# Half of the modulation's weight sums moved from TensorE to VectorE, the norms' squares added up before TensorE sees them, and GpSimd's subtraction cut in four

## The reference, cut to what matters

```python
c_act = silu(c)                                  # [1, 1024]
mod = c_act @ w_ada + b_ada                      # [1, 9216]
sh1, sc1, g1, sh2, sc2, g2, sh3, sc3, g3 = split(mod, 9)
u = rmsnorm(h, norm_ffn1) * (1 + sc1) + sh1
h = h + 0.5 * g1 * swiglu(u, w_ffn1_up, w_ffn1_down)     # f1, f1d
u = rmsnorm(h, norm_mix) * (1 + sc2) + sh2
h = h + g2 * hybrid_mixer(u, ...)                        # convolutions, gated delta rule
u = rmsnorm(h, norm_ffn2) * (1 + sc3) + sh3
h = h + 0.5 * g3 * swiglu(u, w_ffn2_up, w_ffn2_down)     # f2, f2d
h = rmsnorm(h, norm_final)
# second network: differential attention, squared-relu MLP m0, mLSTM, MLP m1, each behind an rmsnorm
# rmsnorm(x, w) = x / sqrt(mean(x * x) + 1e-6) * w
```

## Time and profile before

| | |
|---|---|
| median of 3 runs | 1561.55 us (1560.59 to 1565.43) |
| the profiled execution | 1560.52 us, its span 1558.4 us |
| TensorE busy | 1454.0 us, 93% of the span |
| VectorE busy | 977.7 us, 63% |
| ScalarE busy | 713.5 us, 46% |
| GpSimd busy | 536.7 us, 34% |
| DMA | 258 MB, 166 GB/s in the mean |

### The profile page before, as it was taken

One profiled execution on the slowest core, in us unless ns is written; L12 is line 12 of the kernel. 1 busy time (PEld: TensorE's weight loads), 2 busy tenths in 40 slices (PEclk: granted clock), 3 DMA queues, 4 the chain that ended last, 5 costly groups with the idle time before them and its releaser, 6 DMA issues.

```text
span 1558.4 us, 27943 instructions
## 1 busy us (share of the span) xinstructions
PE 1454.0 (93%) x12009; PEld 1299.8 (83%) x12009; DVE 977.7 (63%) x1301; ACT 713.5 (46%) x1122; POOL 536.7 (34%) x209
## 2 busy tenths in 40 slices
PE   6999999879888899899999989799999998899998
PEld 3888787868777888878888989688999996888998
DVE  4565545868865446575765477569944754789632
ACT  3544534533344334445555546445534455455432
POOL 0444432212121212334444333235543440345542
PEclk9999999979999999999999999899999997999999
DMA  9877676613233443357555544335565551355551
GB/s 360 270 236 254 232 268 198 154 55 116 78 109 137 137 136 109 135 170 238 189 186 191 189 136 150 108 104 186 177 210 168 158 164 53 106 161 185 197 169 49
DMA packets 234441, 258.16 MB, mean 166 GB/s; under 512 B 8457, under 2 KB 211663, under 8 KB 234319
## 3 DMA queue, kind: packets, MB, share of 16 engines
q1 hardware_dynamic: 230272, 252.35, 48.8%
q10 hardware_dynamic: 4047, 4.04, 1.4%
HBM read 253.75 MB, written 2.62 MB: 165 GB/s over the span
## 4 chain that ended last, share of the span: by engine, by line
PE 77%; DVE 15%; ACT 4%; issue 2%; DMA 1%; POOL 0%; DVEq 0%; SPq 0%; ACTq 0%
PE ps L665 30%; PE ps L659 23%; PE ps L661 11%; DVE w_lo L1707 2%; PE ps L632 2%; DVE mt L1907 2%; DVE sil L1907 2%; PE ps L917 2%; PE ps L695 1%; ACT w_hi L1177 1%; DVE cac L2376 1%; DMA raw<-in_w_ada 1%; PE ps L891 1%; PE ps L641 1%; PE ps L880 1%
## 5 line engine op out<-in xcount | busy, mean ns | idle before, releaser
L614 POOL TENSOR_TENSOR w_lo<-raw,w_hi 128x1024 fp32r<-128x1024 f32 (+1 forms) x204 | 536.2, 2630 | 1004.1 <-ACT w_hi L1177 1004.1
L1177 ACT CAST w_hi<-raw 128x1024 fp32r<-128x1024 f32 (+1 forms) x408 | 412.7, 1044 | 205.3 <-PE ps L665 138.5
L659 PE MATMUL ps<-u_hl,w_hi 128*128 128x512 f32 x1216 | 429.6, 398 | 3.9 <-DVE w_lo L1707 1.4
L665 PE MATMUL ps<-u_hl,w_hi 128*128 128x256 f32 x1856 | 364.0, 297 | 23.1 <-DVE w_lo L1707 4.5
L1707 DVE TENSOR_TENSOR w_lo<-raw,w_hi 128x1024 fp32r<-128x1024 f32 x204 | 280.7, 1378 | 134.3 <-ACT w_hi L1177 133.3
L661 PE MATMUL ps<-u_hl,w_lo 128*128 128x256 f32 x1216 | 340.3, 280 | 0.0
L665 PEld LDWEIGHTS ps<-u_hl,w_hi 128*128 128x128 f32 x1856 | 304.3, 201 | 36.7 <-issue 13.9
L659 PEld LDWEIGHTS ps<-u_hl,w_hi 128*128 128x128 f32 x1216 | 228.8, 188 | 66.1 <-issue 11.5
L665 PE MATMUL ps<-u_hl,w_lo 128*128 128x256 f32 x928 | 270.7, 292 | 0.0
L661 PEld LDWEIGHTS ps<-u_hl,w_lo 128*128 128x128 f32 x1216 | 230.0, 189 | 0.1
L665 PEld LDWEIGHTS ps<-u_hl,w_lo 128*128 128x128 f32 x928 | 186.6, 201 | 0.0
(11 more groups left out here) (365 smaller groups left out, 1687.1 us busy)
## 6 DMA issues: line engine op xcount, KB each, us to landing
raw<-in_mlp_w SPq DMA_DIRECT2D x64, 1024.0 KB, 5.2
raw<-in_w_ffn_up SPq DMA_DIRECT2D x44, 1024.0 KB, 5.1
raw<-in_w_ada SPq DMA_DIRECT2D x36, 1024.0 KB, 7.3
raw<-in_w_in SPq DMA_DIRECT2D x30, 1024.0 KB, 5.0
raw<-in_w_ffn_down SPq DMA_DIRECT2D x16, 1024.0 KB, 5.4
raw<-in_attn_w_in SPq DMA_DIRECT2D x12, 1024.0 KB, 4.9
raw<-in_mlstm_w_in SPq DMA_DIRECT2D x12, 1024.0 KB, 5.1
raw<-in_w_ffn_down SPq DMA_DIRECT2D x8, 768.0 KB, 4.2
```

The costliest lines, as they stand in the source:

```text
L614: pool.tensor_tensor(w_lo[half][:, 0:k, :], src, w_hi[half][:, 0:k, :].bitcast(F32), ALU.subtract).then_inc(low_ready(n, h)[0], 1)
L659: pe.matmul(two(b - 10 + m), x, z, start=(first and kt == ks.start), stop=False, skip_group_check=True)
L665: mm = pe.matmul(bank(b)[:, m * S:(m + 1) * S], a, z[c] if type(z) is tuple else z[:, c, :], start=(first and m == 0 and kt == ks.start an ...
L1177: act.copy(w_hi[t % HALVES][:, 0:k, :], src).then_inc(hi_ready, 1)
```

## The change

There are three parts.

**1. Nine pairs on VectorE.** For pairs 4 to 11 and 17 (`BY_VECTOR`) TensorE no longer makes `ada_sums`. VectorE forms the same sum in `rows(p, a)`: for each of the four blocks of a transfer it multiplies a 128 x 512 piece of `raw` by one column of `cpad` and adds it to `arow`, four dependent instructions per transfer. TensorE's `mod_sums` then waits for `row_sums` in place of ScalarE's copy, and SyncE waits for `row_sums` before it refills the buffer. In the up steps pair p is now due one step earlier (`ADA`: steps 0, 2, 4, 6, 8), its first half is added up in that step, the second in the next, and `mod_sums` follows in the one behind.

**2. Squares added by VectorE.** `summed(name, c)` adds the squares of blocks 2c, 2c + 1 into those of blocks 0, 1. TensorE then sums two blocks for `attn`, `mlp0`, `mlstm` and `mlp1`, and four (0, 1, 6, 7) for `ffn1`, `mix`, `ffn2` and `final2`, all in one place, behind the last group or behind the next stage's first slab.

**3. GpSimd in four pieces.** The subtraction of a half slab, one instruction of 128 x 1024, becomes four of 128 x 256.

```diff
@@ Plan.ada
-        self.group("ada", p)
+        if p not in BY_VECTOR:
+            self.group("ada", p)
@@ 
-ADA = {"f1": ({1: 4, 3: 5, 5: 6, 7: 7, 9: 8}, {0: 9, 1: 10, 2: 11, 3: 12}, {1: 9, 2: 10, 3: 11, 4: 12}),
+ADA = {"f1": ({0: 4, 2: 5, 4: 6, 6: 7, 8: 8}, {0: 9, 1: 10, 2: 11, 3: 12}, {1: 9, 2: 10, 3: 11, 4: 12}),
        "f2": ({1: 17}, {}, {})}
+BY_VECTOR = (4, 5, 6, 7, 8, 9, 10, 11, 17)
+BY_TENSOR = (2, 3, 0, 1, 12, 13, 14, 15, 16)
@@ SyncE, load
-                        sp.wait_ge(s("ada_sums"), 2 * turn(m // 2) + m % 2 + 1)
+                        p, a = divmod(m, 2)
+                        if p in BY_VECTOR:
+                            sp.wait_ge(s("row_sums"), 2 * BY_VECTOR.index(p) + a + 1)
+                        else:
+                            sp.wait_ge(s("ada_sums"), 2 * BY_TENSOR.index(p) + a + 1)
@@ GpSimd
-                    pool.tensor_tensor(w_lo[half][:, 0:k, :], src, w_hi[half][:, 0:k, :].bitcast(F32),
-                                       ALU.subtract).then_inc(low_ready(n, h)[0], 1)
+                    for kt in range(k):
+                        op = pool.tensor_tensor(w_lo[half][:, kt, :], src[:, kt, :], w_hi[half][:, kt, :].bitcast(F32),
+                                                ALU.subtract)
+                    op.then_inc(low_ready(n, h)[0], 1)
@@ TensorE, ffn
-                    if i in ups:
-                        ada_sums(ups[i])
-                    if i - 1 in ups:
-                        mod_sums(ups[i - 1])
+                    if i - 2 in ups:
+                        mod_sums(ups[i - 2])
...
-                    if g:
-                        squares(then, g - 1)
                     if g in mods:
                         mod_sums(mods[g])
-                    if g in downs:
+                    if g == 3 and g in downs:
                         ada_sums(downs[g])
                 if then not in LATE:
-                    squares(then, 3)
+                    squares(then)
@@ VectorE
+            def rows(p, a):
+                r = arrived(dve, ("ada", 2 * p + a))
+                if a == 0:
+                    dve.wait_ge(s("mod_sums"), turn(p) - 1)
+                row = row_at(p)
+                for k in range(4):
+                    x, c = raw4[r][:, k, :], cpad[:, 4 * a + k, 0:1]
+                    op = (dve.scalar_tensor_tensor(row, x, c, row, mul, add) if a or k else
+                          dve.tensor_scalar(row, x, c, None, mul))
+                    if k < 3:
+                        link(op)
+                op.then_inc(s("row_sums"), 1)
+                dve.wait_ge(s("row_sums"), 2 * BY_VECTOR.index(p) + a + 1)
...
+            def summed(name, c):
+                if c == 0 or c == 3 and name not in LATE[:-1]:
+                    return
+                dve.wait_ge(s("sq_ready"), 4 * NORMS.index(name) + c + 1)
+                op = dve.tensor_tensor(uf[:, 0:2, :], uf[:, 0:2, :], uf[:, 2 * c:2 * c + 2, :], add)
+                if name == "attn":
+                    op = dve.tensor_tensor(sq2[0], sq2[0], sq2[c], add)
...
@@ VectorE, ffn
                     dve.tensor_tensor(mt, sil, sil2, mul).then_inc(s("mid_f"), 1)
+                    if i in ups:
+                        rows(ups[i], 0)
                     if i - 1 in ups:
-                        mod_out(ups[i - 1])
+                        rows(ups[i - 1], 1)
+                    if i - 2 in ups:
+                        mod_out(ups[i - 2])
...
                         ahead(plan.slab[(name + "d", g, q)])
+                        if q < 2 and g and g - 1 in downs:
+                            rows(downs[g - 1], q)
...
+                        if q == 2 and g:
+                            summed(then, g - 1)
@@ VectorE, attention
                 ahead(plan.slab[("aqkv", 0)] + 1)
+                summed("attn", 3)
                 root("attn")
```

More of the change, by code:

```diff
@@ L684, in warm, with squares @@
                     pe.matmul(bank(7), cs("ident"), cst[:, 0:512], start=True, stop=True, skip_group_check=True)
-            def squares(norm, c):
+            def squares(norm):
                 v = NORMS.index(norm)
-                pe.wait_ge(s("sq_ready"), 4 * v + c + 1)
-                for k in (2 * c, 2 * c + 1):
+                pe.wait_ge(s("sum_ready"), v + 1)
+                for k in (0, 1) if norm in LATE[:-1] else (0, 1, 6, 7):
+                    if k == 6:
+                        pe.wait_ge(s("sq_ready"), 4 * v + 4)
+                    last = k == (1 if norm in LATE[:-1] else 7)
                     if norm == "final2":
@@ L730, in columns @@
                     if due and j == 0:
-                        squares(due, 3)
-                    if then and j:
-                        squares(then, j - 1)
+                        squares(due)
                 if pair:
@@ L771, in _ @@
             ada_sums(3)
-            for c in range(4):
-                squares("ffn1", c)
+            squares("ffn1")
             pe.wait_ge(s("params_in"), 16 * NPAR)
@@ L1071, in attention @@
                     if i == 0:
-                        squares("attn", 3)
+                        squares("attn")
                 for part in range(2):
@@ L1087, in attention @@
                             out_turned(1)
-                        elif c:
-                            squares("mlp0", c - 1)
             def mlstm():
@@ L1159, in _ @@
             mlp("m1", "mlp1", "final2")
-            squares("final2", 3)
+            squares("final2")
             turned_out(3)
@@ L1849, in _ @@
                 square(c)
+            for c in (1, 2):
+                summed("ffn1", c)
             dve.wait_ge(s("prm_T"), 1)
```

39 lines of the change are left out of this document (24 added, 15 removed).

## The result

| | median | runs | profiled span | TensorE clock |
|---|---|---|---|---|
| before, beside it | 1561.55 us | 3 | 1558.4 us | 0.963 |
| after | 1595.7 us | 4 | 1592.8 us | 0.957 |

The ratio is 1.0222, interval 1.0203 to 1.0241: 2.2% slower, against a forecast of 1557 us and a range up to 1583. A fourth run of before, at 3551.66 us, was disturbed and is left out.

What follows compares the result with a forecast made beforehand. TensorE, 93% busy, was taken to bound the kernel. Terms +11 (ups), +8 (downs), +2 (second network), -11.5 (squares), -14 (pieces) sum to -4.5 on 1560.52 us: 1556, stated as 1557 against the median; range 1532 to 1583.

Steps and rivals of the forecast that it cites:

- Up steps: First network's up steps: waits on VectorE and loads add 22.2 us, pairs' sums removed save 10.9; +11 us.
- the slack of 2.2 us: Up step: `w_lo` done at T+3.3, TensorE wants it at T+5.54, T being an up slab's end.
- The lower bound of -7: Up steps' best case: no exclusion between VectorE and GpSimd and faster transfers, 3.6 - 10.9 = -7 us.
- hidden: Rival: VectorE's sums are hidden, up steps win 7 us, down groups 5 to 8; 1525 us, up to 1540; chance 0.20.
- the distances of `lowp`: Sign in the up steps: 7.9 to 8 us where VectorE adds a second half, not 5.54.
- Down groups: First network's down groups: late buffer release makes a 22.3 us load loop, and pair 12 arrives late; +8 us.
- Second network: Pair 17, two calls on VectorE: 2.1 + 2.4 - 2.17, so +2 us; bounds -2, +4.
- Squares: Norms outside `ffn1`: -17.0 us of TensorE work, against +3.4 at the attention's entry and 2.1 elsewhere; -11.5 us.
- Pieces: GpSimd's pieces shorten VectorE's waits: 8 us in the mixer, 8 at attention and entries, 2 lost; -14 us.
- The loads decide: Rival: SyncE's queue in the first network sets the time, up +19, down +14, pieces nothing; 1585 us; chance 0.18.
- pieces bring nothing: Rival: convolutions run in fours, so each wait is only cut up; 1571 us; chance 0.17.

Runs made afterwards that it cites:

- e6: e1 with only the last of the four VectorE instructions of each half pair issued; 1558.1 us, ratio 0.9994 to before.
- e5: e1 with VectorE's sums reading constants in SBUF and each pair's buffer reused once its transfer has landed; 1589.7 us, ratio 1.0179 to before.
- e1: Before with only the sums of pairs 4 to 11 and 17 on VectorE, squares and GpSimd's subtraction unchanged; 1614.4 us, ratio 1.0348.
- e7: e1 with the second half of each up-step pair summed behind the second slab's low part, not behind `mt`; 1581.2 us, ratio 1.0129 to before.
- e2: Before with only the squares added by VectorE as in the change; 1560.9 us, ratio 1.0015.
- e10: e2 with TensorE multiplying the last block itself for `attn`, `mlp0`, `mlstm` and `mlp1`; 1550.7 us, ratio 0.9944 to before.
- e3: Before with only GpSimd's subtraction cut into four pieces; 1547.0 us, ratio 0.9913.
- e16: e10 plus GpSimd's four pieces, with the squares of `ffn1` and `mlp0` left whole to TensorE; 1542.8 us, ratio 0.9884 to before.
- e12: e7 plus GpSimd's subtraction in four pieces, no squares by VectorE; 1563.8 us, ratio 1.0028 to before.

## Why the prediction was wrong, by its own steps

**Up steps: +11, measured +30.** The mechanism was right, VectorE and GpSimd by turns and a low part late, and so was its size at odd steps (2.4 a call, measured 2.4 to 2.6). Two things were missing. First, at even steps and step 0 I had 1.4 and 2.1, and 2.5 for the loads, 10.2 in all; 29.4 idle less 12.7 at the odd ones leaves 16.7, with waits of 5.33 and 4.45 us in two steps whose slab was late. Second, a term that the sum did not have at all: what TensorE loses beyond the waits, 11.3 us, of which 8.6 is the lower clock behind five of the eleven waits and 2.6 the pairs around them. 19.7 + 2.5 - 10.9 = 11.3 becomes 29.4 + 11.3 - 10.9 = 29.8.

**The step that failed is this sum.** It put TensorE's loss at its waits alone, with nothing for the clock, and had the waits of the even steps 6.5 us too low: 18.5 of the 39 us by which the whole was off. The squares' entry (below) is the next largest, 13.5.

**A second misreading is the slack of 2.2 us.** It hardly moved the forecast, which priced the turns with GpSimd, but it moved the bounds. I took `w_lo` as free to move within it. Its margin was not against TensorE but against GpSimd, 0.54 us; e6 shows it lost with a single instruction. I had seen `mid_hl` take 2.89 us there and had not asked what it would mean for `w_lo` to stand in its place. The lower bound of -7 rested on there being no exclusion, and so did the rival "hidden". Of the signs, the distances of `lowp` at odd steps were 8.2 to 8.4 us, and once 10.0, not 7.9 to 8: the pairs around the waits, and in the last case the lower clock.

**Down groups: +8, measured +13.** The loop of loads was right, 22.3 forecast. ScalarE's `w_hi` in after, this stretch:

```profile
248.38 3.49 ACT L1181 CAST w_hi<-raw 128x1024 fp32r<-128x1024 f32 x4 [9.89 <-DMA raw<-in_w_ffn_down]
...
260.03 2.00 ACT L1181 CAST w_hi<-raw 128x1024 fp32r<-128x1024 f32 x2 [8.17 <-DMA raw<-in_w_ffn_down]
...
270.74 3.59 ACT L1181 CAST w_hi<-raw 128x1024 fp32r<-128x1024 f32 x4 [8.71 <-DMA raw<-in_w_ffn_down]
...
292.15 0.58 ACT L1204 COPY arow<-ps 128x512 f32<-128x512 f32 x1 [7.55 <-PE ps L641]
```

22.36 us lie between the first and the third, and pair 12 arrives late, as said. e5 confirms the cause by taking it away. It also shows the rest of the miss: e1 and e5 make the same products in the downs, but TensorE is busy 78.3 us in e1, at a clock of 0.92, and 71.7 in e5, at 1.00. Of e1's 17.5 us over e5, 6.5 are thus that same missing term.

**Second network: +2, measured +8 (e1).** e7, which moved only the second half of pair 17 there, has +3. The same mis-sized place, and two low parts late.

**Squares: -11.5, measured +2.** The entry of the attention was named but put at 3.4. In e2 the addition fell behind a whole GpSimd subtraction, TensorE then idled 8 us, and its clock fell: net 2 lost 4 where it should have gained. In after, with the pieces, the two additions took 1.21 us each as forecast, yet `rms` comes 9.7 us behind the stage's first `w_lo`, where before has 4.1: 5.6 later, not 3.4, since TensorE had idled 6.3 us and made the last products at the lower clock.

```profile
932.68 1.21 DVE L1744 TENSOR_TENSOR uf<-uf 128x512 f32<-128x512 f32 x1
933.81 1.21 DVE L1746 TENSOR_TENSOR sq<-sq,sq 128x512 f32<-128x512 f32 x1
938.89 0.47 ACT L1213 ACTIVATE rms<-ps,cc 128x256 f32<-128x256 f32 x1 [5.61 <-PE ps L714]
```

The sum also took the start as free of cost (0); in e2 it is 5 us longer. Cut out of the entries (e10) they bring -9, near the forecast.

**Pieces: -14, measured -13.6 (e3),** in the mixer 5 of the 8 forecast, in the attention and at entries the rest. Right in size and mostly in place, though it was called the least certain. That measured size is the whole's; of its places, the mixer's 5 is within what one stage of one execution can vary, and the means of nine (e16) give 6. VectorE's sums that met a piece each took 1.05 us (four in 4.18), not 1.15.

**The rivals.** "The loads decide" had the right sign and stage and the best number (1585), but its place holds alone only in the downs; in the up steps the turns with GpSimd cost as much once the loads are early (e5). "Hidden" is excluded by e1, "pieces bring nothing" by e3. The terms of e1, e2 and e3 add to +43 and the changed kernel has +35: the parts are not independent, perhaps since pieces soften what the sums collide with (17 us gained in e12, 13.6 in e3); that is not shown.

## What to carry to other kernels

When work goes to another engine, do not ask only how long it is free, but which of its instructions started just ahead of GpSimd's, and by how much: here a margin of 0.5 us, once lost, cost a whole GpSimd instruction. Cut the long instruction of the engine that is not the bound: that alone gave 0.9%. If TensorE begins to wait, count its clock too: here 8.6 us on top of 29 of waits in one stage. And move a last dependent step off a stage's entry, even when each step is small.
